# The scan stage of a two-block model: eight pair iterations become sixteen single-direction units, stepped one behind the other

## The reference, cut to what matters

```python
def rwkv7_scan(r, w, k, v, kk, a):
    def step(state, inp):
        r_t, w_t, k_t, v_t, kk_t, a_t = inp
        sa = jnp.einsum('bhvk,bhk->bhv', state, -kk_t)
        state = (state * w_t[:, :, None, :] + sa[..., None] * (kk_t * a_t)[:, :, None, :]
                 + v_t[..., None] * k_t[:, :, None, :])
        return state, jnp.einsum('bhvk,bhk->bhv', state, r_t)
...
for d in range(2):
    ...
    ins = [rh, heads(decay), kd, vh, kk, heads(a)]
    if d == 1:
        ins = [jnp.flip(t, axis=1) for t in ins]
    o = rwkv7_scan(*ins)
    ...
    bonus = jnp.sum(rh * kd * r_k, axis=-1, keepdims=True) * vh
    dir_out.append((group_norm(o, gn_w, gn_b) + bonus) * g)
```

## Time and profile before

| | us |
|---|---|
| median of three runs | 2948.64 |
| the profiled execution's own time | 2948.97 |
| its span in the trace | 2947.2 |
| PE busy | 2581.6 |
| DVE busy | 1421.7 |
| ACT busy | 1205.1 |
| POOL busy | 871.9 |

### The profile page before, as it was taken

One profiled execution on the slowest core, in us unless ns is written; L12 is line 12 of the kernel. 1 busy time (PEld: TensorE's weight loads), 2 busy tenths in 40 slices (PEclk: granted clock), 3 DMA queues, 4 the chain that ended last, 5 costly groups with the idle time before them and its releaser, 6 DMA issues.

```text
span 2947.2 us, 48727 instructions
## 1 busy us (share of the span) xinstructions
PE 2581.6 (88%) x19252; PEld 1798.9 (61%) x19252; DVE 1421.7 (48%) x2378; ACT 1205.1 (41%) x2270; POOL 871.9 (30%) x501
## 2 busy tenths in 40 slices
PE   4999979999969967787777787779999799999999
PEld 2876648888724436666665666348788476683443
DVE  4026532011092157776876777143931369873302
ACT  3236633233241146765676665133643222236011
POOL 2310134444310033433342322044444343331103
PEclk9999989999989979898999999889999899999999
DMA  2221012232202200000000000212532223332222
GB/s 104 86 67 50 20 50 86 86 101 89 95 29 79 70 6 8 8 8 3 8 8 9 2 3 2 72 43 86 192 115 92 78 93 122 100 93 72 71 79 71
DMA packets 49749, 180.81 MB, mean 61 GB/s; under 512 B 5584, under 2 KB 5712, under 8 KB 49296
## 3 DMA queue, kind: packets, MB, share of 16 engines
q1 hardware_dynamic: 45920, 166.98, 18.0%
q10 hardware_dynamic: 3632, 11.08, 1.0%
HBM read 167.49 MB, written 10.55 MB: 60 GB/s over the span
## 4 chain that ended last, share of the span: by engine, by line
PE 70%; DVE 10%; issue 9%; ACT 7%; POOL 3%; DMA 0%; DVEq 0%; POOLq 0%; SPq 0%; ACTq 0%
PE ps L534 15%; PE ps L530 11%; PE ps L531 11%; PE ps L532 11%; PE ps L682 4%; PE ps L624 2%; ACT arena L1180 2%; PE ps L604 2%; POOL h L1880 2%; ACT arena L1174 2%; PE ps L553 2%; POOL ring_lo L1867 1%; PE ps L701 1%; PE ps L612 1%; PE ps L909 1%
## 5 line engine op out<-in xcount | busy, mean ns | idle before, releaser
L1867 POOL TENSOR_TENSOR ring_lo<-ring,ring_hi 128x1024 fp32r<-128x1024 f32 x198 | 495.9, 2512 | 735.9 <-ACT ring_hi L960 735.9
L534 PE MATMUL ps<-arena,ring 128*128 128x512 f32 x1024 | 452.5, 602 | 43.5 <-DVE arena L1586 19.3
L531 PE MATMUL ps<-u_lo,ring_hi 128*128 128x512 f32 x968 | 386.0, 399 | 0.0
L534 PEld LDWEIGHTS ps<-arena,ring 128*128 128x128 f32 x1024 | 196.3, 193 | 298.2 <-issue 279.6
L682 PE MATMUL ps<-arena 128*64 128x64 f32 x4480 | 193.0, 239 | 66.6 <-ACT arena L1180 64.7
L960 ACT ACTIVATE ring_hi<-ring 128x1024 fp32r<-128x1024 f32 x198 | 207.2, 1052 | 75.8 <-DMA ring<-in_wall 72.1
L682 PEld LDWEIGHTS ps<-arena 128*64 128x64 f32 x4480 | 179.1, 152 | 89.3 <-issue 88.6
L530 PE MATMUL ps<-mlp_u_hi,ring_hi 128*128 128x512 f32 x512 | 204.5, 399 | 20.6 <-DVE u_lo L1399 20.6
L531 PEld LDWEIGHTS ps<-u_lo,ring_hi 128*128 128x128 f32 x968 | 184.3, 190 | 42.4
L532 PE MATMUL ps<-mlp_u_hi,ring_lo 128*128 128x512 f32 x512 | 203.6, 398 | 0.0
L530 PE MATMUL ps<-mid_hi,ring_hi 128*128 128x512 f32 x512 | 202.6, 396 | 0.3 <-POOL ring_lo L1867 0.3
(11 more groups left out here) (440 smaller groups left out, 5222.5 us busy)
## 6 DMA issues: line engine op xcount, KB each, us to landing
ring<-in_wall SPq DMA_DIRECT2D x273, 512.0 KB, 3.6
s_tables<-arena ACTq DMA_DIRECT2D x16, 512.0 KB, 3.3
arena<-s_tables SPq DMA_DIRECT2D x16, 512.0 KB, 3.6
arena<-bias_lines SPq DMA_DIRECT2D x16, 448.0 KB, 4.4
arena<-in_lora SPq DMA_DIRECT2D x8, 384.0 KB, 3.1
h<-in_x SPq DMA_DIRECT2D x1, 2048.0 KB, 7.8
out<-arena ACTq DMA_DIRECT2D x8, 256.0 KB, 2.8
consts<-in_consts SPq DMA_DIRECT2D x1, 1378.0 KB, 10.8
```

Of the source, the lines that this page charges most:

```text
L531: nc.tensor.matmul(y, w_hi, low, start=False, stop=False)
L534: mm = nc.tensor.matmul(bank((t0 + j) % 2), ring[:, at:at + P], rhs(x), start=x == 0, stop=x == k - 1)
L1867: G.tensor_tensor(ring_lo[:, slot], ring[:, slot], ring_hi[:, slot].bitcast(F32), ALU.subtract).then_inc(sem("weights_split"), 1)
```

## The change: what it does, and the diff

The scan stage goes unit by unit (pair 0 direction 0, pair 0 direction 1, pair 1 direction 0, and so on). A new function `slot` on every engine takes four units at once: `k`, whose scores and levels are computed; `s`, the unit before it, whose 8 scan steps are put between the pieces of `k`; `o`, the unit before that, whose output is finished; and `f`, the unit after `k`, whose features are made. Steps 0 to 2 of the scan stand between the scores, steps 3 to 7 in the five levels. There are 16 slots with a `k`, and one more that has only scan steps and output.

Further edits. `level_product` makes a level's product with 8 matmuls in place of 16: the moving operand takes the columns of both heads from the two pads at once, and only the half of the columns that is new at this level (`cut`); its output lies turned with regard to its input. The ScalarE and VectorE operations on it take half columns too. The copy into `TT` becomes one half-width activation (it was four of 64x256). `each_turned` is now 16 matmuls with the identity in place of 4 transposes, and its result is taken by one full copy in place of four. The starting `TT` is a turned copy of `T` in place of two GpSimd operations. The state is no longer pre-multiplied on VectorE: a matmul with the identity (`eye`) adds the old state in PSUM, and VectorE only scales. The reciprocal is cut into two halves.

```diff
+            def level_product(out, a, pad, l, h):
+                of = pad.rearrange("p (e m b h w) -> p e m b h w", e=2, m=NCH, h=2, w=1 << l)
+                for m in range(NCH):
+                    rows, block = slice(m % 2 * CH, (m % 2 + 1) * CH), slice(m // 2 * P, (m // 2 + 1) * P)
+                    to = out[rows, block].rearrange("p (e b h w) -> p e b h w", e=2, h=2, w=1 << l)
+                    mm = nc.tensor.matmul(to[:, :, :, h, :], a[:, m * CH:(m + 1) * CH], of[:, :, m, :, h, :],
+                                          start=True, stop=True)
...
+                def scan_w(j):
...
+                        pe.wait_ge(sem("state_ready"), unit(s, 7, j))
...
+                        nc.tensor.matmul(C[q][rows, 0:CH], S["ka"][:, at], v_alone[e][:, at], start=True, stop=False)
+                        if j:
+                            nc.tensor.matmul(C[q][rows, 0:CH], const("eye", 0, CH), s_alone[j % 2][q][e],
+                                             start=False, stop=False)
...
+                scan_w(0)
+                if k:
+                    pe.wait_ge(sem("features_p"), unit(k, 1, 1))
+                    pe.wait_ge(sem("spread"), unit(k, 2, 1))
+                    each(A[d], F["be"], r["al_alone"]).then_inc(sem("scores_ready"), 1)
+                    pe.wait_ge(sem("spread"), unit(k, 2, 2))
+                    if o:
+                        pe.wait_ge(sem("o_copied"), unit(o, 1, 1))
+                    each(O[d], F["ka"], r["ro_alone"]).then_inc(sem("scores_ready"), 1)
+                scan_u(0)
+                if k:
+                    each(C[d], F["ka"], r["al_alone"]).then_inc(sem("scores_ready"), 1)
+                scan_s(0)
+                scan_w(1)
+                if k:
+                    pe.wait_ge(sem("n_copied"), unit(k, 1, 1))
+                    each_turned(B[d], r["N"]).then_inc(sem("scores_ready"), 1)
+                    each(A[d], F["be"], r["ro_alone"]).then_inc(sem("scores_ready"), 1)
+                scan_u(1)
+                if f:
+                    hidden_out(f, 0)
+                scan_s(1)
+                scan_w(2)
+                if k:
+                    turned_blocks(C[d], r["T"]).then_inc(sem("tt_ready"), 1)
+                if f:
+                    pe.wait_ge(sem("z_taken"), unit(f, 3, 1))
+                    hidden_out(f, 1)
+                scan_u(2)
+                if o:
+                    if f:
+                        pe.wait_ge(sem("z_taken"), unit(f, 3, 2))
+                    out_mean(o, Q)
+                scan_s(2)
+                for l in range(1, LEVELS):
+                    scan_w(l + 2)
+                    level_x(l)
+                    scan_u(l + 2)
+                    level_t(l)
+                    scan_s(l + 2)
+                    if l < LEVELS - 1:
+                        level_turn(l)
+                    if o and l == 1:
+                        out_bonus(o, Q)
+                    if o and l == 2:
+                        out_variance(o, Q)
+                    if f and l == 3:
+                        if o:
+                            pe.wait_ge(sem("deviation"), unit(o, 1, 1))
+                        hidden_out(f, 2)
+                if k:
+                    each_turned(C[d], F["ka"]).then_inc(sem("scores_ready"), 1)
+                    each_turned(A[d], F["be"]).then_inc(sem("scores_ready"), 1)
+                    if d == 0:
+                        each_turned(B[d], v_st).then_inc(sem("scores_ready"), 1)
```

ScalarE, the level part of its slot:

```diff
+                for l in range(1, LEVELS):
+                    scan_w(l + 2)
+                    if k:
+                        level_x(l)
+                        if l < LEVELS - 1:
+                            level_turn(l)
+                    if f and l == 1:
+                        decays(f, E)
+                    if o and l == 2:
+                        out_square(o, Q)
+                    if o and l == 3:
+                        out_deviation(o, Q)
+                    if f and l == 3:
+                        spread_al(f, E)
+                    if f and l == 4:
+                        gate_in(f, E)
```

VectorE, the level part of its slot:

```diff
+                for l in range(1, LEVELS):
+                    scan_u(l + 2)
+                    if k:
+                        level_t(l)
+                    scan_s(l + 2)
+                    if k and l < LEVELS - 1:
+                        level_pad(l)
+                    if o and l == 2:
+                        out_bonus(o, Q)
+                    if f and l == 2:
+                        decayed(f, E, f_ends)
+                    if o and l in (3, 4):
+                        out_inverse(o, Q, l - 3)
+                if o:
+                    out_scaled(o, Q)
```

More of the change, by code:

```diff
@@ L704, in out_means @@
[L704 to L717, removed]
@@ L1277, in _, with decay_in @@
-            first, last = (lambda per, c=0: c), (lambda per, c=0: (DT - 1) * per + c)
-            for step in range(3):
-                features(first, feats[0], step)
-            for d in range(2):
-                decays(first, feats[0], d)
-            for k in range(4):
-                spread(first, feats[0], k)
+            def decay_in(f, F):
+                n, d = f
+                act.wait_ge(sem("z_ready"), unit(f, 3, 1))
+                nc.scalar.activation(F["al"], bank(4 * (1 - d) + 3), ACT.Sigmoid, bias=pair_col("w0", n, d)
+                                     ).then_inc(sem("z_taken"), 1)
@@ L1740, in _ @@
+            def pair(parity, n, prev, nxt):
+                G, H = feats[parity], feats[1 - parity]
+                here, there = p_end[parity], p_end[1 - parity]
+                slot((n, 0), G[0], (prev, 1) if prev else None, H[1], (prev, 0) if prev else None, H[0], (n, 1), G[1],
+                     there, here)
+                slot((n, 1), G[1], (n, 0), G[0], (prev, 1) if prev else None, H[1], (nxt, 0) if nxt else None, H[0],
+                     here, there)
             first, last = (lambda per, c=0: c), (lambda per, c=0: (DT - 1) * per + c)
-            for step in range(4):
-                features(first, feats[0], p_end[0], step)
+            decay_sums((first, 0), feats[0][0])
@@ L1748, in _ @@
+            out_bonus((last, 1), G[1])
+            for part in range(2):
+                out_inverse((last, 1), G[1], part)
+            out_scaled((last, 1), G[1])
             post_norm(5, ("norm_g", 5 * DT), kTr)
@@ L1922, in _, with pair @@
+            def pair(parity, n, prev, nxt):
+                here, there = feats[parity], feats[1 - parity]
+                slot((n, 0), (prev, 1) if prev else None, (n, 1), here[1])
+                slot((n, 1), None, (nxt, 0) if nxt else None, there[0])
+            first = lambda per, c=0: c
             for a in alone_a + alone_b + [v_alone]:
@@ L1972, in _ @@
-            first = lambda per, c=0: c
-            stage_v(first)
-            for step in range(2):
-                features(first, feats[0], step)
+            rates((first, 0), feats[0][0])
+            scaled_keys((first, 0), feats[0][0])
             over_pairs(pool, pair)
```

816 lines of the change are left out of this document (395 added, 421 removed).

## The result

The changed kernel takes 2986.34 us (median of four runs, 2975.88 to 2997.65) against 2948.47 for the one before (four runs, 2947.25 to 2954.58): ratio 1.0125, 95% interval 1.0083 to 1.0167. It is slower by 37.9 us, where 17 were forecast. The profiled execution took 2990.23 us, 41.3 more than the profiled one of before; its mean granted clock is 0.942, and the four runs of the new kernel stand in the order of theirs: 0.950, 0.947, 0.942, 0.940 for 2975.88, 2982.45, 2990.23, 2997.65.

The account below looks back on a forecast made before the run. The prediction took hand-offs between engines, none full, to bound the scan stage. Front -15.4, middle +11.3 and back +20.9 made +16.8 us on 2948.97, so 2966 us, range 2893 to 3012.

Parts of the forecast that it names:

- D: Rival that is the forecast itself: slower by the interleaving's own waits, 2955 to 2990 us; chance 0.40.
- The walk along PE's queue: Step-by-step sum of a slot's scan steps and levels: 46.1 us direction 1, 47.4 direction 0, mean 46.75.
- clock term: Addition to a slot for lower granted clock, chiefly levels 2 and 3: 1.5 us, between 0 and +5.
- restart share: Loop restart, PE waiting and then running slowly: about 5 us, three times, 1.3 us for each of twelve slots.
- The ends of the stage: Front 89.6 us after against 105 before, -15.4; back 132.1 against 111.2, +20.9.
- The waits named: PE waits: level 2 exponentials +2.9 us and variance on DVE's bonus +1.5; level 3 hidden product on square root 2.7.
- The engines: Busy time for a unit: DVE falls from 35.9 to 28.8 us, ACT from 32.7 to 25.6; none near full.
- Unknown prices: Half-column additions taken at 0.4 us (0.34 to 0.69), a strided `level_product` at 0.5 (up to 1.0).
- The Trainium skill's rule: Drain of about 1.38 us beside each 1.28 us ACT table load, some 60 us over the stage; not used.
- A: Rival: the change wins as ACT and DVE slack shrinks PE's waits in levels 2 and 3; 2898 us, chance 0.35.
- C: Rival: thinly spread PE work keeps the levels at 1.2 GHz, +3 us a slot, 3010 us; chance 0.12.
- B: Rival: no change within 0.2%, 2949 us, clock and hand-off terms 1.1 us a slot lower; chance 0.13.

Follow-up runs that it names:

- The state's experiment: Kernel before, with only the old state added in PSUM by an identity matmul and VectorE just scaling it: 2940.53 us, ratio 0.9974.
- Side by side: Kernel before in its own order, both directions together, with all parts of the change but the interleaving: 2872.52 us; with unread products too, 2858.18 us.

## Why the prediction was right or wrong

The direction, the mechanism (D) and the range hold; 2986.3 lies in the narrow range of D too (2955 to 2990). The size was off: 37.9 against a forecast of 17.3 (2966 less 2948.64), by terms that can be named.

**The walk along PE's queue, without its clock term, was right to 1%, in part by luck.** It gave 46.75 and a restart share of 1.3: 48.05. With the clock up the middle is 572.99 / 12 = 47.75. Direction 1 at a clock of 1.00 took 45.9 for 46.1, and level by level 4.7, 8.3, 7.4 and 3.8 for 4.7, 8.1, 7.4 and 3.8: here the walk was right in its parts. In the kernel with unread products direction 0 took 48.2 to 49.0 for 47.4: the addition of the turned `v` was put at 1.3 and is over 2. Against that the restart of the loop was put at three times 5 us; the wait stands twice in the middle, in both kernels (3.8 each before, 4.27 and 4.43 after), and with the clock up it makes some 0.5 a slot for 1.3. These two misses nearly cancel.

**The step that failed: "I take 1.5" for the clock.** The runs show 2.7 a slot, 32.8 in the middle and 35.2 in all, where 1.5 is 18 in the middle; that is 14 of the 20 us. I had both ends, +5 and 0, and took the value nearer the rows of before. I looked for the loss in levels 2 and 3 alone, with PE busy 6.6 of 15.5 us there; it is 8.7 of 15.7 at full clock. The slot at 0.86 is 3.8 longer than the one at 1.00, and 2.7 of that (18.38 for 15.68) stand in those two levels: the low clock lasts beyond them, and in them it meets full products, the variance (2.04 for 1.12) and a hidden product (2.08 for 1.12). Why it falls in some slots and not in others with the same waits stays open.

**The ends of the stage.** Front 93.1 for 89.6; its clock is 0.79. Back 140.3 for 132.1: the last two slots with a `k` 91.6 for 88.5, the slot with only a scan 29.5 for 28, and the last output with the landing of the weights 19.2 for 15.6. PE waits there for a DMA into the ring, 11.39 us, in the kernel before 15.07. The front window of after, and the last two parts of the back (here cut at 1887.50, 0.7 us ahead of the last output mean):

```profile
1068.26:1161.32 93.06, 63.38 (x1122) 48.25 (x1123) 38.88 (x84) 47.88 (x95) 31.47 (x25) 0.79 0.02 6
...
1858.73:1887.50 28.77, 18.98 (x270) 13.10 (x270) 13.40 (x36) 5.19 (x19) 0.00 (x0) 0.85 0.00 1
1887.50:1907.38 19.88, 6.25 (x7) 1.53 (x7) 9.25 (x11) 1.91 (x3) 0.00 (x0) 0.50 0.14 46
```

The misses sum to 11.2 (middle) + 3.5 + 8.2 + 2.2 (later start) = 25.1 on a forecast of 16.8.

**The waits named were the waits found.** The u behind the exponentials: 2.04. The variance: its wait is there (1.08 to 1.44), but in nine of twelve slots the last to release it was ACT's square (L1286) and not DVE's bonus, as named. The hidden product of level 3 on the root: 2.47 for 2.7. The table loads were priced at their 1.28 each, 3.84 a slot, and with the clock up they are worth 3.65 a slot: that price held. What the sum had too low is the clock beside them, and the runs tie the two together: without the loads it came back from 0.90 to 0.99.

**The engines.** 328.5 / 12 = 27.4 us of DVE and 25.1 of ACT a slot, for 28.8 and 25.6. **Unknown prices.** A `level_product` takes 0.69 with its last result, so 0.5 it was, and no cost of the strided operand shows; a half-column addition takes 0.42 for 0.40. **The Trainium skill's rule** on what a table load costs ("ScalarE: Activation LUTs", What ACT_TABLE_LOAD costs) asked for a drain beside the load: the 24 loads at the exponentials and the root have 0.4 us idle in all ahead of them, and the load that starts at 1448.33 ends 0.01 before the root starts. No drain is seen, and the row was the one to follow.

**Rivals.** A fell: ACT and DVE did get their slack, and PE waited for them in the same places. Taking the loads off (80 us) and setting another order in level 3 (9.6) do bring what A hoped for, so the slack is worth something once the queue's order lets it through. C named the cause of the miss with too high a price: 3 a slot on top of the 1.5 where 1.2 was missing, and a clock of 0.90, not under 0.8, in the middle. B, no change, fell with the interval. One reading ahead of the sum was wrong too: that in the scan phase DVE "is nearest to full" and so sets the step. The state's experiment took a third of its work there away and won 0.08 us a step.

## What to carry to other kernels

Before two chains are interleaved in queues that run in order, list for every operation with a long lead (a table load, a root) which short operation stands behind it on its engine and who waits for that; the sum of these waits, rather than the load of the engines, is most of what the order cost here in the middle of the stage; the ends, where nothing stands beside the first and the last unit, cost 27 us more here. Then look at what PE does behind each long wait: full products there may run at the lower clock, as the variance did in eight slots of twelve. Where a wait can't be removed, unread products in it may be cheaper than the clock that it costs, but only as long as the wait covers them.

## What the runs showed of the hardware that was not expected

- Work that nobody reads made three kernels faster: by 35.2, 18.7 and 14.3 us, with the granted clock of the middle at 0.99 where it had been 0.90, 0.92 and 0.89.
- The granted clock goes with the spread of the new kernel's runs: 22 us, in the order of 0.950 to 0.940. Side by side with unread products the spread is 4.5.
- The clock can differ between two slots with the same instructions and the same waits of 2.03, 1.44 or 1.08, and 2.47 us: 1.00 and 45.9 us in one, 0.86 and 49.7 in another.
- A table load costs what it delays: 48 in the stage cost 80 us by units (45 of them with the clock up), 23 cost 3.4 side by side.
- No cost of strided half columns in PSUM shows: the 8 matmuls of a `level_product` take 0.69 with their last result where 16 took some 1.2 (two sets 2.37), and an addition of 128x256 takes 0.42 where 128x512 took 0.69.
